# Second and third feed forward of a two-block layer stack: the up products with x held still and 512 weight columns moving, gated results turned on TensorE, and borders that go by quarters of x

## The chip, the core and the metric

The kernel runs on one core of one Trainium2 chip. A core has TensorE (PE in the profile; its weight loads are listed as PEld), VectorE (DVE), ScalarE (ACT), GpSimd (POOL) and SyncE (SP, which here only issues DMA). The metric is the device time of one execution in microseconds. The kernel before has a median of 3593.2 us over 3 runs (3590.34 to 3593.96).

## What is computed

Two blocks run one after the other on 256 rows (tokens) of 2048 columns, all in float32. The first block has a conditioned Fourier and mLSTM mixer and a feed forward with a convolution. The second has a feed forward, a mixer (a state space model beside sparse attention) and another feed forward. The change touches the two feed forwards of the second block, `f1` and `f2` below, called the second and the third feed forward of the kernel (n = 1 and n = 2):

```python
D_MODEL, SEQ, D_FF = 2048, 256, 5632

def _rmsnorm(x, g):
    xf = x.astype(jnp.float32)
    ms = jnp.mean(xf * xf, axis=-1, keepdims=True)
    return (xf * lax.rsqrt(ms + EPS)).astype(x.dtype) * g

def _swiglu(x, wg, wu, wd):
    return (jax.nn.silu(x @ wg) * (x @ wu)) @ wd

# second_block, the lines that matter here
f1 = _swiglu(_rmsnorm(h, ffn1_pre_g[l]), ffn1_w_gate[l], ffn1_w_up[l], ffn1_w_down[l])
h = h + 0.5 * _rmsnorm(f1, ffn1_post_g[l])
...
h = h + _rmsnorm(mixed, mix_post_g[l])
f2 = _swiglu(_rmsnorm(h, ffn2_pre_g[l]), ffn2_w_gate[l], ffn2_w_up[l], ffn2_w_down[l])
h = h + 0.5 * _rmsnorm(f2, ffn2_post_g[l])
```

## The kernel before

**Products in three parts.** Each float32 operand is split into a rounded part (`w_hi`, `xt_hi`, `hid_hi`) and the rest (`w_lo`, `xt_lo`, `hid_lo`). A product is hi·hi + hi·lo + lo·hi, three passes over the array.

**Weights stream in units of 1 MB.** A unit is 128 x 2048 elements. SP loads it into one of four slots of `stage`. ACT copies it to `w_hi` (`split`, L792), DVE subtracts to get `w_lo` (L1303), and both land in one of two halves of the split buffers. ACT may start on a unit only when PE has used up the unit two before it (`split_used`), and PE may start on a unit when DVE is done with it (`split_made`). SP reloads a slot when its unit is split. The order of the units is fixed by a plan that is worked out when the program is built (`plan[name]`, with the index of the first unit of each stage).

**The feed forward.** The 5632 hidden columns are 44 chunks of 128. They are done in two parts, 24 and 20 chunks (`PARTS`): the up products of a part (`up10`, `up11` of the second feed forward, `up20`, `up21` of the third), and then its down product (`down10` and so on). In the up products of before one unit holds 128 columns of the gate weights, or of the up weights, for all 2048 rows: 16 k chunks of 128 x 128. Two units, gate and up, make a pair, and there are 44 pairs in each feed forward. The weights are the stationary operand and x, turned so that its columns lie on the partitions, is the moving one (`wide_steps`):

```python
pe.matmul(dst, wh, both(k), start=k == 0, stop=False)                     # 512 columns: x_hi and x_lo of 256 rows
last = pe.matmul(dst[:, T:2 * T], wl, chunk(xt_hi, k), start=False, stop=False)  # 256 columns
```

The result is already turned: hidden columns on partitions and rows along the free axis, as the down product needs it. For each pair ACT copies a half of the banks (`e0`, L877), DVE adds the other (`d0`, L1499), multiplies by the row's reciprocal root, which was laid out along the free axis in `rsb` (`d1`, L1509), ACT takes the Silu (`e2`, L892), DVE multiplies gate and up (`d2`, L1532), and ACT and DVE split the result into `hid_hi` and `hid_lo` (`e3`, `d3`). Pairs run in hardware loops.

**The down product** (`rows_half`) has the other form: 128 rows of the turned hidden tile are stationary and 512 weight columns move; a unit is 256 rows of weights by 1024 columns. It is 24 matmuls of 512 columns a unit. Its last unit goes by quarters of the output (`quarters`, L2322 to L2324), so that the norm that follows can start on the first quarter.

**The borders.** Before the second feed forward the rows of x are made from the last down product of the first (`down01`), quarter by quarter: DVE (`add_gated`, `weigh_final`), then PE turns them (`norm(2, ...)`, L2384), and ACT and DVE scale and split them into `xt_hi` and `xt_lo` (`scaled_hi` L857, `scaled_lo` L1354). Before the third, the output product of the mixer (`out2`) has to be complete for its norm (`post_tail`); then `new_x(6, q)` (L1445) makes a quarter of x, `norm(4)` turns it, and so on. A unit of before needs all of x. `norm_done` counts the eight groups (two k chunks each) of x that are ready.

**The bias tables.** In the second feed forward PE also makes the bias tables of the attention (`bias_rows`, L2427 and L2431, 62 small matmuls); DVE copies them out (`take_bias`), and GpSimd writes them to memory with 16 transfers, of which each waits for a given number of used units.

## Time and profile before

| what | value |
|---|---|
| median of 3 runs | 3593.2 us |
| profiled execution: its time, its span | 3594.03 us, 3592.1 us |
| PE busy | 3425.2 us, 95% |
| PEld busy | 2919.4 us, 81% |
| DVE busy | 2130.7 us, 59% |
| ACT busy | 1636.2 us, 46% |
| granted TensorE clock, mean | 0.97 |
| second feed forward, up products of part one | from 1260.13 to 1553.45 us |
| third feed forward, first up matmul | 2836.82 us |

The table says how full each engine is, and where the two feed forwards lie. Busy time of PE comes from matmuls whose ends are modelled and overlap, so the spacing of starts, not the mean duration, is what one reads for its pace. A granted clock of 1.00 is 2.4 GHz, and 0.50 is 1.2 GHz.

### The profile page before, as it was taken

Reading aid. Unit: us, or ns where it says so; the run is one execution under the profiler, and the core shown is the slowest. Engines: PE = TensorE matmul, PEld = TensorE weight load, DVE = VectorE, ACT = ScalarE, POOL = GpSimd, SP = SyncE. Lnnn points to the kernel's source line nnn. Section 1 sums busy time; section 2 is a strip of 40 time slices with the busy share of each in tenths; the row PEclk is TensorE's granted clock in tenths of the full one; section 3 lists DMA queues with packets and bytes.
Section 4 is the critical chain, followed back from the end, with each engine's and each line's share of the span. In section 5 each row is a group of like instructions: output and inputs, shape, how many; then the busy total and the mean of one; then the engine's idle time right before and its main releaser. Section 6 shows DMA issues by size and latency. Waiting matters only on the chain.

```text
span 3592.1 us, 49777 instructions
## 1 busy us (share of the span) xinstructions
PE 3425.2 (95%) x19694; PEld 2919.4 (81%) x19694; DVE 2130.7 (59%) x2280; ACT 1636.2 (46%) x1772; POOL 346.2 (10%) x411
## 2 busy tenths in 40 slices
PE   5899889999999999999999899999999899999998
PEld 1786678888888888888888799898888788888886
DVE  0774657775566565544555578895455555545555
ACT  0333346653455455543443455663443555434443
POOL 1110000000000000000000147661000000000000
PEclk7899999999999999999999999999899999999999
DMA  9998657776666667976665656667235566666664
GB/s 398 297 340 299 221 167 225 225 227 221 188 187 195 189 186 164 204 206 189 187 187 188 175 149 156 168 179 232 91 106 187 153 187 186 187 189 188 185 188 139
DMA packets 813373, 712.54 MB, mean 198 GB/s; under 512 B 13127, under 2 KB 742527, under 8 KB 805696
## 3 DMA queue, kind: packets, MB, share of 16 engines
q1 hardware_dynamic: 787840, 627.09, 58.9%
q0 software_dynamic: 20624, 79.44, 7.8%
q10 hardware_dynamic: 4784, 4.27, 0.4%
q8 instruction: 88, 1.44, 0.2%
q14 instruction: 37, 0.30, 0.0%
HBM read 698.94 MB, written 11.80 MB: 198 GB/s over the span
## 4 chain that ended last, share of the span: by engine, by line
PE 78%; DVE 9%; ACT 4%; DMA 4%; issue 3%; POOL 1%; ACTq 0%; DVEq 0%; SPq 0%; POOLq 0%
PE ps L2267 24%; PE ps L2268 12%; PE ps L2335 8%; PE ps L2336 8%; PE ps L2339 8%; DVE w_lo L1303 3%; ACT w_hi L792 3%; DMA stage<-in_w_ada 2%; PE ps L2286 2%; PE ps L2287 2%; PE ps L2288 2%; PE ps L2265 2%; PE ps L2299 1%; PE ps L2495 1%; PE ps L2300 1%
## 5 line engine op out<-in xcount | busy, mean ns | idle before, releaser
L1303 DVE TENSOR_TENSOR w_lo<-stage,w_hi 128x2048 fp32r<-128x2048 f32 x528 | 1221.4, 2313 | 1093.7 <-ACT w_hi L792 1092.6
L792 ACT ACTIVATE w_hi<-stage 128x2048 fp32r<-128x2048 f32 x528 | 1010.8, 1914 | 1483.5 <-PE ps L2265 617.0
L2267 PE MATMUL ps<-xt,w_hi 128*128 128x512 f32 x3960 | 1416.2, 400 | 11.3 <-DVE w_lo L1303 10.1
L2268 PE MATMUL ps<-xt,w_lo 128*128 128x256 f32 x3960 | 1114.1, 281 | 0.0
L2267 PEld LDWEIGHTS ps<-xt,w_hi 128*128 128x128 f32 x3960 | 746.9, 189 | 187.8 <-DVE w_lo L1303 14.5
L2268 PEld LDWEIGHTS ps<-xt,w_lo 128*128 128x128 f32 x3960 | 750.9, 190 | 11.8
L2335 PE MATMUL ps<-w_hi,hid_hi 128*128 128x512 f32 x1152 | 449.2, 390 | 5.8 <-DVE w_lo L1303 5.8
L2336 PE MATMUL ps<-w_lo,hid_hi 128*128 128x512 f32 x1152 | 448.2, 389 | 0.0
L2286 PE MATMUL ps<-xt,w_hi 128*128 128x256 f32 x1184 | 342.2, 289 | 18.9 <-DVE w_lo L1303 16.6
L2339 PE MATMUL ps<-w_hi,hid_lo 128*128 128x512 f32 x1152 | 354.7, 389 | 0.0
L2287 PE MATMUL ps<-xt,w_hi 128*128 128x256 f32 x1184 | 337.0, 285 | 0.0
L2288 PE MATMUL ps<-xt,w_lo 128*128 128x256 f32 x1184 | 336.8, 284 | 0.0
L2335 PEld LDWEIGHTS ps<-w_hi,hid_hi 128*128 128x128 f32 x1152 | 216.2, 188 | 52.4 <-DVE w_lo L1303 4.3
L2286 PEld LDWEIGHTS ps<-xt,w_hi 128*128 128x128 f32 x1184 | 229.0, 193 | 29.8 <-issue 23.6
L2339 PEld LDWEIGHTS ps<-w_hi,hid_lo 128*128 128x128 f32 x1152 | 216.2, 188 | 45.0
L2336 PEld LDWEIGHTS ps<-w_lo,hid_hi 128*128 128x128 f32 x1152 | 216.3, 188 | 44.7
L2287 PEld LDWEIGHTS ps<-xt,w_hi 128*128 128x128 f32 x1184 | 229.3, 194 | 0.0
L2288 PEld LDWEIGHTS ps<-xt,w_lo 128*128 128x128 f32 x1184 | 229.1, 193 | 0.0
L2335 PE MATMUL ps<-w_hi,xt 128*128 128x512 f32 x248 | 98.4, 397 | 8.7 <-issue 3.2
L2265 PE MATMUL ps<-xt,w_hi 128*128 128x512 f32 x264 | 105.4, 399 | 0.0
L2495 PE MATMUL ps<-stage,csilu 128*32 128x512 f32 x384 | 68.3, 808 | 33.6 <-DMA stage<-in_w_ada 33.1
L2336 PE MATMUL ps<-w_lo,xt 128*128 128x512 f32 x248 | 97.2, 392 | 0.0
(414 smaller groups left out, 3649.9 us busy)
## 6 DMA issues: line engine op xcount, KB each, us to landing
stage<-in_w_in SPq DMA_DIRECT2D x92, 1024.0 KB, 5.7
stage<-in_w_up SPq DMA_DIRECT2D x88, 1024.0 KB, 5.8
stage<-in_ffn_w_gate SPq DMA_DIRECT2D x88, 1024.0 KB, 5.6
stage<-in_ffn_w_up SPq DMA_DIRECT2D x88, 1024.0 KB, 5.6
stage<-in_ffn_w_down SPq DMA_DIRECT2D x88, 1024.0 KB, 5.5
stage<-in_w_ada SPq DMA_DIRECT2D x48, 1024.0 KB, 8.8
stage<-in_w_down SPq DMA_DIRECT2D x44, 1024.0 KB, 5.1
late<-in_w_ada POOLq DMA_DIRECT2D x64, 512.0 KB, 6.7
```

The lines of the kernel that those rows point to most:

```text
L792: act.activation(w_hi[:, u % 2 * UNIT:(u % 2 + 1) * UNIT], slot(u % SLOTS), ACT.Copy).then_inc(hi_made, 1)
L1303: dve.tensor_tensor(w_lo[:, part], slot(u % SLOTS), w_hi[:, part].bitcast(F32), ALU.subtract).then_inc(split_made, 1)
L2265: last = pe.matmul(dst, wh, both(k), start=False, stop=True)
L2267: pe.matmul(dst, wh, both(k), start=k == 0, stop=False)
L2268: last = pe.matmul(dst[:, T:2 * T], wl, chunk(xt_hi, k), start=False, stop=False)
L2286: pe.matmul(dst, wh, chunk(xh, k0 + k), start=start and k == 0, stop=False)
L2287: pe.matmul(dst, wh, chunk(xl, k0 + k), start=False, stop=False)
L2288: last = pe.matmul(dst, wl, chunk(xh, k0 + k), start=False, stop=stop and k == n - 1)
L2335: pe.matmul(rows_cols(half, m, n, 512, swapped), a, wh, start=st, stop=False)
L2336: pe.matmul(rows_cols(half, m, n, 512, swapped), a, wl, start=False, stop=False)
L2339: last = pe.matmul(rows_cols(half, m, n, 512, swapped), b, wh, start=False, stop=en)
L2495: last = pe.matmul(ps[32 * j:32 * j + 32, b * 512:(b + 1) * 512], weight.to_broadcast([P, 32]), part[:, j % 2 * 512:(j % 2 + 1) * 512], st ...
```

## The change

It does four things in the second and third feed forward; the first feed forward keeps its form.

1. The up products take the form of the down product. A unit now holds 512 columns of gate (or up) weights for 4 k chunks (`blocks_of`). A block is 512 hidden columns, 8 units: gate and up in turn, for the four quarters of x. `BLOCKS` gives 6 and 5 blocks for the two parts, so there are still 88 units in each feed forward. In a unit each 128 x 128 piece of x is stationary and 512 weight columns move, 24 matmuls (`unit`). Results have rows on the partitions. A block takes four PSUM banks, and two blocks alternate.
2. The gating is done by block: Silu with the row's reciprocal root as scale (`gate`, ACT, 2 instructions), one product on DVE (`product`, 2 instructions), then PE turns the product, 8 transposes of 128 x 128 (`turn_hid`), after the second unit of the next block, and ACT and DVE split it (`hidden`, 2 instructions each). The layout of the root along the free axis goes (`rs_rows`, `take_rs`, `rsb`).
3. The borders go by quarters of x: the first two units need only its first quarter, and the transposes of the other quarters stand between the units (`norm_ffn1`, `norm_ffn2`). The orders on DVE and ACT follow.
4. The bias tables are made after unit 28 of `up10` (it was unit 11), and the loops over pairs and over the halves of the down product are written out.

```diff
+BLOCKS = tuple(chunks // 4 for _, chunks in PARTS)
...
+        def blocks_of(ws, f0):
+
+            views = [w.rearrange("(c k p) n -> c p k n", p=P, k=4) for w in ws]
+            return lambda i, u: [(slot(u % SLOTS).rearrange("p (k n) -> p k n", k=4),
+                                  views[u % 2][u // 2][:, :, ds(i * 512 + f0 * P, 512)])]
...
+                def gate(j):
+
+                    act.wait_ge(S["norm_rs"], ROOT_AT[RS_ROOT[n]] + 1)
+                    act.wait_ge(split_used, plan[up][1] + 8 * j + 9)
+                    for m in range(MT):
+                        at = RS_COL[n] + m
+                        last = act.activation(turn[:, m * 512:(m + 1) * 512], bank(block_bank(j, 0, m)), ACT.Silu,
+                                              scale=stats[:, at:at + 1])
+                    last.then_inc(S["pair_e2"], 1)
...
+                    if j and u == 0:
+                        gate(j - 1)
+                    elif j and u == 3:
+                        hidden(j - 1)
...
+                def product(j):
+
+                    dve.wait_ge(S["pair_e2"], block_at(n, part, j) + 1)
+                    dve.wait_ge(split_used, plan[up][1] + 8 * j + 10)
+                    for m in range(MT):
+                        at = RS_COL[n] + m
+                        last = dve.scalar_tensor_tensor(out=h_blk[:, m * 512:(m + 1) * 512],
+                                                        in0=bank(block_bank(j, 1, m)), scalar=stats[:, at:at + 1],
+                                                        in1=turn[:, m * 512:(m + 1) * 512], op0=ALU.mult, op1=ALU.mult)
+                    last.then_inc(S["pair_d2"], 1)
...
+                def unit(v):
+
+                    j, u = divmod(v, 8)
+                    pe.wait_ge(split_made, plan[up][1] + v + 1)
+                    for kk in range(4):
+                        k, at = 4 * (u // 2) + kk, v % 2 * UNIT + kk * 512
+                        wh, wl = (w[:, at:at + 512] for w in (w_hi, w_lo))
+                        for m in range(MT):
+                            dst = bank(block_bank(j, u % 2, m))
+                            pe.matmul(dst, chunk(xt_hi, k, m), wh, start=k == 0, stop=False)
+                            pe.matmul(dst, chunk(xt_hi, k, m), wl, start=False, stop=False)
+                            last = pe.matmul(dst, chunk(xt_lo, k, m), wh, start=False, stop=k == KC - 1)
+                    last.then_inc(split_used, 1)
+
+                def turn_hid(j):
+
+                    pe.wait_ge(S["pair_d2"], block_at(n, part, j) + 1)
+                    for c in range(4):
+                        for m in range(MT):
+                            last = pe.transpose(bank(block_bank(j, 0, c // 2), c % 2 * T + m * P, P),
+                                                h_blk[:, m * 512 + c * P:m * 512 + (c + 1) * P], ident[:, :])
+                    last.then_inc(S["hid_turned"], 1)
...
+                    unit(v)
+                    if part == 0 and j == 0:
+                        between(u)
+                    if j and u == 1:
+                        turn_hid(j - 1)
+                    if n == 1 and part == 0 and v == 28:
+                        bias_rows()
...
         def enter_ffn1(split):
 
             split(0)
+            square_pieces(2, x_nat, 1, 0, 4, 4)
             split(1)
-            square_pieces(2, x_nat, 1, 0, 4)
+            square_pieces(2, x_nat, 2, 0, 4, 6)
+            split(2)
             scaled_hi(2, 4, C_F1)
             scaled_hi(2, 5, C_F1)
...
-            new_x(6, 0)
-            new_x(6, 1)
-            scaled_lo(4, 0, C_F2)
-            scaled_lo(4, 1, C_F2)
-            split(1)
...
+            for q in range(4):
+                new_x(6, q)
+                if q == 3:
+                    dve.sem_inc(S["x_made"], 1)
+                scaled_lo(4, 2 * q, C_F2)
+                scaled_lo(4, 2 * q + 1, C_F2)
+                split(q + 1)
```

On PE, in the up products of the second feed forward, the order of before at the end of a unit and the start of the next is as follows (`xt` moves over `w_hi` or `w_lo`; L2267 is the matmul of 512 columns, L2268 that of 256, and L2264 and L2265 are those two of the last k chunk).

```order
L2268 MATMUL ps<-xt,w_lo 128x256
L2267 MATMUL ps<-xt,w_hi 128x512
L2268 MATMUL ps<-xt,w_lo 128x256
L2264 MATMUL ps<-xt,w_lo 128x256
L2265 MATMUL ps<-xt,w_hi 128x512
```

At the second unit of a block of the changed kernel, with the transposes of the block before, PE has these rows (L2581 to L2583 are the three passes of `unit`, L2591 is `turn_hid`).

```order
L2581 MATMUL ps<-w_hi,xt 128x512
L2582 MATMUL ps<-w_lo,xt 128x512
L2583 MATMUL ps<-w_hi,xt 128x512
L2591 MATMUL ps<-ident,h_blk 128x128 [waits pair_d2]
L2591 MATMUL ps<-ident,h_blk 128x128 x7
L2581 MATMUL ps<-w_hi,xt 128x512 [waits split_made]
L2582 MATMUL ps<-w_lo,xt 128x512
```

So all matmuls of a unit move 512 columns, and eight transposes that wait for DVE's product stand between two units once a block.

On DVE, at the start of the third feed forward, the order of before is this (L1445 is `new_x`, L1354 `scaled_lo`, L1303 the split of a unit).

```order
L1445 SCALAR_TENSOR_TENSOR x_nat<-f_nat,stats,x_nat 128x512 x4
L1354 SCALAR_TENSOR_TENSOR xt<-ps,cols,xt 128x256 x4
L1303 TENSOR_TENSOR w_lo<-stage,w_hi 128x2048
L1445 SCALAR_TENSOR_TENSOR x_nat<-f_nat,stats,x_nat 128x512 x2
L1354 SCALAR_TENSOR_TENSOR xt<-ps,cols,xt 128x256 x4
L1445 SCALAR_TENSOR_TENSOR x_nat<-f_nat,stats,x_nat 128x512 x2
L1354 SCALAR_TENSOR_TENSOR xt<-ps,cols,xt 128x256 x8
L1319 TENSOR_REDUCE stats<-stats 128x2
L1323 TENSOR_SCALAR stats<-stats 128x2
L1303 TENSOR_TENSOR w_lo<-stage,w_hi 128x2048
```

The same place in the changed kernel (L1509 is `new_x`, L1423 `scaled_lo`, L1372 the split):

```order
L1509 SCALAR_TENSOR_TENSOR x_nat<-f_nat,stats,x_nat 128x512 x2
L1423 SCALAR_TENSOR_TENSOR xt<-ps,cols,xt 128x256 x4
L1372 TENSOR_TENSOR w_lo<-stage,w_hi 128x2048
L1509 SCALAR_TENSOR_TENSOR x_nat<-f_nat,stats,x_nat 128x512 x2
L1423 SCALAR_TENSOR_TENSOR xt<-ps,cols,xt 128x256 x4
L1372 TENSOR_TENSOR w_lo<-stage,w_hi 128x2048
L1509 SCALAR_TENSOR_TENSOR x_nat<-f_nat,stats,x_nat 128x512 x2
L1423 SCALAR_TENSOR_TENSOR xt<-ps,cols,xt 128x256 x4
L1372 TENSOR_TENSOR w_lo<-stage,w_hi 128x2048
L1509 SCALAR_TENSOR_TENSOR x_nat<-f_nat,stats,x_nat 128x512 x2
L1423 SCALAR_TENSOR_TENSOR xt<-ps,cols,xt 128x256 x4
L1372 TENSOR_TENSOR w_lo<-stage,w_hi 128x2048 x2
```

Before, all four quarters were made with one split in between; now each quarter is made, scaled and followed by the split of one unit.

## Rows read from the trace of the kernel before

**Rows 1.** Page, part 1: busy us, share of the span, instructions.

```profile
PE 3425.2 (95%) x19694; PEld 2919.4 (81%) x19694; DVE 2130.7 (59%) x2280; ACT 1636.2 (46%) x1772; POOL 346.2 (10%) x411
```

**Rows 2.** Page, part 4: the chain that ended last, by engine.

```profile
PE 78%; DVE 9%; ACT 4%; DMA 4%; issue 3%; POOL 1%; ACTq 0%; DVEq 0%; SPq 0%; POOLq 0%
```

**Rows 3.** Groups by line: busy us, mean ns | idle before, releaser.

```profile
L2267 PE MATMUL ps<-xt,w_hi 128*128 128x512 f32 x3960 | 1416.2, 400 | 11.3 <-DVE w_lo L1303 10.1 <-issue 1.2
```

**Rows 4.** Timeline of PE, one unit of `up10`: start us, duration us.

```profile
1547.80 0.40 PE L2267 MATMUL ps<-xt,w_hi 128*128 128x512 f32 x1
...
1553.45 0.40 PE L2335 MATMUL ps<-w_hi,hid_hi 128*128 128x512 f32 x1
```

**Rows 5.** Timeline of PE, last unit of `down01` and the matmul after it.

```profile
1254.69 0.39 PE L2322 MATMUL ps<-w_hi,hid_hi 128*128 128x512 f32 x1
...
1260.13 0.39 PE L2267 MATMUL ps<-xt,w_hi 128*128 128x512 f32 x1
```

**Rows 6.** Timeline of PE, four transposes between two units of `down01`.

```profile
1242.39 0.62 PE L2339 MATMUL ps<-w_hi,hid_lo 128*128 128x512 f32 x2
1242.84 0.60 PE L2384 MATMUL ps<-ident,f_nat 128*128 128x128 f32 x4
1243.20 0.48 PE L2335 MATMUL ps<-w_hi,hid_hi 128*128 128x512 f32 x1
1243.52 0.39 PE L2336 MATMUL ps<-w_lo,hid_hi 128*128 128x512 f32 x1
```

**Rows 7.** Groups by line, 1400 to 1500 us, in `up10`.

```profile
L1303 DVE TENSOR_TENSOR w_lo<-stage,w_hi 128x2048 fp32r<-128x2048 f32 x18 | 41.3, 2292 | 43.7 <-ACT w_hi L792 43.7
L792 ACT ACTIVATE w_hi<-stage 128x2048 fp32r<-128x2048 f32 x18 | 34.5, 1916 | 46.5 <-PE ps L2265 46.5
...
L1499 DVE TENSOR_TENSOR turn<-turn,ps 128x512 f32<-128x512 f32 x9 | 6.1, 680 | 0.0
L877 ACT ACTIVATE turn<-ps 128x512 f32<-128x512 f32 x9 | 5.2, 577 | 0.0
...
L892 ACT ACT_TABLE_LOAD x4 | 5.1, 1283 | 0.1
```

**Rows 8.** Timeline of PE, start of the second feed forward: third and fourth unit.

```profile
1278.32 0.50 PE L2267 MATMUL ps<-xt,w_hi 128*128 128x512 f32 x1 [1.79 <-DVE w_lo L1303]
...
1289.83 0.39 PE L2265 MATMUL ps<-xt,w_hi 128*128 128x512 f32 x1
```

**Rows 9.** Timeline of DVE at the same border.

```profile
1265.29 1.28 DVE L1387 TENSOR_TENSOR f_nat<-ps,row 128x512 f32<-128x512 f32 x2
...
1267.93 1.29 DVE L1400 TENSOR_TENSOR f_nat<-x_nat,wf_row 128x512 f32<-128x512 f32 x2
```

**Rows 10.** Timeline of ACT at the same border.

```profile
1262.21 0.61 ACT L807 ACTIVATE turn<-x_nat 128x512 f32<-128x512 f32 x1
```

**Rows 11.** Timeline of DVE at the start of the third feed forward.

```profile
2823.32 2.86 DVE L1445 SCALAR_TENSOR_TENSOR x_nat<-f_nat,stats,x_nat 128x512 f32<-128x512 f32 x4
2826.88 1.66 DVE L1354 SCALAR_TENSOR_TENSOR xt<-ps,cols,xt 128x256 fp32r<-128x256 f32 x4 [0.70 <-ACT xt L857]
```

**Rows 12.** Timeline of PE there: first up matmuls, last matmul of unit four.

```profile
2836.82 0.78 PE L2267 MATMUL ps<-xt,w_hi 128*128 128x512 f32 x1
...
2838.25 0.63 PE L2267 MATMUL ps<-xt,w_hi 128*128 128x512 f32 x1
...
2840.81 0.57 PE L2267 MATMUL ps<-xt,w_hi 128*128 128x512 f32 x1
...
2863.28 0.40 PE L2265 MATMUL ps<-xt,w_hi 128*128 128x512 f32 x1
```

**Rows 13.** Windows: length, busy of PE, PEld, DVE, ACT, POOL, then PEclk, DMA share.

```profile
1210.00:1300.00 90.00, 84.97 (x425) 70.28 (x424) 66.20 (x69) 49.27 (x65) 7.61 (x13) 1.00 0.67 192
...
2837.00:2840.00 3.00, 3.00 (x11) 2.52 (x11) 1.73 (x4) 2.95 (x6) 0.00 (x0) 0.50 0.00 0
```

**Rows 14.** DMA issues: transfers of the bias tables, KB each, us to landing.

```profile
rev_scratch<-rev_sb POOLq DMA_DIRECT2D x16, 192.0 KB, 8.9
```

More of the change, by code:

```diff
@@ L890, in e2 @@
                     act.wait_ge(S["pair_d1"], j + (q0 + 3))
-                    src = conv_a[:, s * T:(s + 1) * T] if conv else turn[:, s * 512:s * 512 + T]
-                    act.activation(conv_a[:, s * T:(s + 1) * T], src, ACT.Silu).then_inc(S["pair_e2"], 1)
+                    here = conv_a[:, s * T:(s + 1) * T]
+                    act.activation(here, here, ACT.Silu).then_inc(S["pair_e2"], 1)
                 def e3(j, s):
@@ L903, in ffn, with ffn_rows, hidden @@
                     split_down(u)
+                    if part:
+                        after(u)
+        def ffn_rows(n, enter, after):
+            for part, (f0, chunks) in enumerate(PARTS):
+                up, down = f"up{n}{part}", f"down{n}{part}"
+                def gate(j):
[6 more added lines that the diff above has]
+                    last.then_inc(S["pair_e2"], 1)
+                def hidden(j):
+                    act.wait_ge(S["hid_turned"], block_at(n, part, j) - FC + 1)
+                    for b in range(2):
+                        at = (4 * j + 2 * b) * T
+                        act.activation(hid_hi[:, at:at + 512], bank(block_bank(j, 0, b)), ACT.Copy).then_inc(S["pair_e3"], 1)
+                for v in range(8 * BLOCKS[part]):
+                    if part or v > 4:
+                        split(up, 0, 0, v)
+                    elif v == 0:
+                        enter(lambda u: split(up, 0, 0, u))
+                    j, u = divmod(v, 8)
+                    if part == 0 and v == 5:
+                        root(RS_ROOT[n], 4 if n == 1 else 2)
+                    if j and u == 0:
+                        gate(j - 1)
+                    elif j and u == 3:
+                        hidden(j - 1)
+                for u in range(chunks):
+                    split(down, 0, 0, u)
+                    if u == 0:
+                        gate(BLOCKS[part] - 1)
+                    elif u == 3:
+                        hidden(BLOCKS[part] - 1)
                     if part:
@@ L1489, in ffn @@
                 pb = PAIR_BANK[part]
-                gating = n == 0 and part == 0
+                gating = part == 0
                 def split_down(u):
@@ L2471, in ffn @@
                     first_pairs()
-                if n == 1 and part == 0:
-                    pairs(1, 3)
-                    bias_rows()
-                    pairs(3, chunks // 2)
-                else:
-                    pairs(part == 0, chunks // 2)
-                if n == 0 and part:
+                pairs(part == 0, chunks // 2)
+                if part:
                     pe.wait_ge(S["mod_made"], 6)
                 rows_phase(f"down{n}{part}", chunks // 2, hid_hi, hid_lo, part == 0, q0 + 2, last=part == 1,
-                           after=turn_early if n == 0 and part else nothing)
+                           after=turn_early if part else nothing)
```

298 lines of the change are left out of this document (173 added, 125 removed).

## The prediction

> **What bounds the kernel now.** I read the page first. PE is busy 95% of the span, DVE 59%, ACT 46% [rows 1], and the chain that ended last runs through PE for 78% of its length [rows 2]. The groups by line then say where PE's own waits are: the matmuls of the up products, 3960 pairs, were held up 11.3 us in all [rows 3]. So inside the feed forwards PE never starves, and what counts is how long PE takes for a unit, and what it does beside units. The groups of a stretch inside `up10` say the same from the other side: ACT stood idle 46.5 us of 100 waiting for PE to free a buffer, and DVE 43.7 us waiting for ACT [rows 7]. Only at the borders does PE wait for the others.
>
> PE's pace I read from starts in its timeline, since the durations overlap. A unit of up products is 32 matmuls, and the starts at its two ends are 1547.80 and 1553.45: 5.65 us [rows 4]. The last unit of a down product goes in exactly the order that the changed `unit` has (hi·hi, hi·lo, lo·hi on one 128 x 128 piece of activations, 512 weight columns moving), and takes from 1254.69 to 1260.13: 5.44 us for 24 matmuls [rows 5]. Both move 12,288 columns (16 x 768 and 24 x 512).
>
> **1. The units.** 88 units in each of two feed forwards go from 5.65 to 5.44 us. That is 0.21 us each, and 176 x 0.21 = 37 us less. ACT's and DVE's part of a unit stays as it is: 1.92 + 2.29 = 4.21 us from the free buffer to the ready unit [rows 7], under the 5.44 us that PE needs for the unit in between. 1.2 us of slack are left, 0.2 less than before.
>
> The Trainium skill (TensorE: Matmul & The Clock Gate, section "Back-to-back issue gap") gives a warm matmul of N columns N/2.4 + 2.5 ns. By that a unit of before would take 5.20 us and a new one 5.18 us, the gain on all units would be about 4 us, and the whole sum about 1 us. The rows speak against it: both forms ran in this kernel, and differ by 0.21 us. I go by the rows.
>
> **2. The transposes.** They are new on PE: 8 for each of 22 blocks, 176 in all. Nothing hides them, since PE is the bound. Four such transposes between two units push the next matmuls: L2339's two start at 1242.39, so the next start is due at 1242.84; it comes at 1243.20, and the one after it another 0.32 us later where 0.23 is usual [rows 6]. That is 0.36 + 0.09 = 0.45 us for four. Eight cost between 0.81 us (the 0.09 paid once) and 0.91 us (twice the four). I take 0.91, so 22 x 0.91 = 20 us more; the low end is 18. Their wait for DVE's product costs nothing: gate and up of a block are done when the next block starts, Silu takes two ACT instructions of about 0.6 us, the product two DVE instructions of about 0.7 us (priced by L877 and L1499, the same 512 columns out of PSUM [rows 7]), the product is ready about 6 us into the block, and PE comes to the transposes after 10.9 us. The read-out after them needs four such instructions in all, and the banks are wanted again 6 units after the transposes, over 30 us later.
>
> **3. ACT and DVE** do less: four pairs of before are 16 DVE instructions and 12 on ACT, a block has 4 and 4 of at most the same width of 512. The table loads of 1.28 us each around every second Silu [rows 7] go with the loops, since code that is written out needs the table once. All of this lies beside PE and is priced at nothing. If it came late it would be worth its excess over the slack; see the third rival.
>
> **4. The border before the second feed forward.** Before, unit 0 starts at 1260.13 [rows 5], unit 2 only at 1278.32 after a wait for its split, and unit 3 ends 0.23 us after 1289.83, at 1290.06 [rows 8]. After: unit 0 starts at the same time, and now needs only the first quarter of x. It ends at 1265.6, and eight transposes make that 1266.5. Unit 1's split comes later than before, since ACT has its two squares (0.61 us and a read-out each [rows 10]) ahead of it; I estimate its start at 1262.6, so it is ready at 1266.8. Unit 1 runs to 1272.3. DVE makes the last quarter of x in 3.93 us (1265.29 to 1269.22 before [rows 9]), now 1266.8 to 1270.7; ACT squares and splits unit 2 behind that, ready at 1274.6: PE idles 1.4 us beside its transposes. Units 2 and 3 then run through to 1285.5. That is 4.6 us earlier, of which 4 x 0.21 are counted already: 3.7 us less.
>
> **5. The border before the third.** Before, DVE has the first quarter of x at 2824.7 and the second 1.4 us later (half of the 2.86 us), and the first four scaled pieces at 2828.54 [rows 11]. PE starts units only at 2836.82, with all quarters turned, and ends unit 3 at 2863.52 [rows 12]. It starts at the granted clock of 0.50, 1.2 GHz [rows 13]: from 2838.25 to 2840.81 four pairs take 0.64 us each, and then the clock rises, after some 4.4 us of dense matmuls [rows 12]. After: the first quarter is scaled at the same 2828.54, and unit 0 may start. I give it the same kind of low-clock start, 4.4 to 6 us at nearly double price, so it ends at about 2836.6. Now each further quarter goes through all engines in turn: PE turns it only between units, ACT and DVE scale it, ACT and DVE split a unit, and only then DVE makes the next quarter. Unit 1 ends at 2842.9; the third quarter is made at 2844.4, PE idles 1.5 us; unit 2 ends at 2850.9, the last quarter is made at 2852.3, again 1.5 us; unit 3 ends at 2858.8. That is 4.7 us earlier, 3.8 us beyond what is counted.
>
> **6. The bias tables** cost the same at their new place, tiny matmuls and a spell of half clock behind them. New is that GpSimd's transfers (16 of 192 KB, 8.9 us to landing [rows 14]) wait for unit counts that have mostly passed by then, so some six go at once. Weight loads have several units of slack by their slots; I price it at 0, at most 4 us.
>
> **Sum.** -37 (units) + 20 (transposes) - 3.7 - 3.8 (borders) = -25 us. The profiled execution took 3594.0 us (span 3592.1 and 1.9 around it), 0.8 above the median. 3594.0 - 25 = 3569, and 3569 stands for the median too.
>
> **Rivals.**
> - *The transposes take the clock down* (the slower side). At the start of the third feed forward, behind transposes that stood alone with gaps, it was 0.50 [rows 13]. Place: after the second unit of a block. A spell of 4.4 us in which a pair takes 0.64 instead of 0.35 us loses 2 us [rows 4, 12], so 22 spells lose 44: 3569 + 44 = 3613. It decides from 1.2 us per block. Against it: the stretch of 1210 to 1300 us has transposes in fours and eights at a granted 1.00 [rows 13]. 0.03. The Trainium skill (the same page, section "Part 4: PE-mode transpose") says transposes do not count as PE-busy in the same way; by that rule the clock would fall only if 0.9 us of them were enough, and here matmuls surround them.
> - *A unit is priced by its columns alone*, and the 0.21 us come from something else in the two places compared. Then units gain nothing, transposes and borders stay: 3594 + 20 - 7.5 = 3606. The equal 12,288 columns speak for it, the measured starts against [rows 4, 5]. 0.03. The skill's gap rule above is the same mechanism with cheaper transposes.
> - *Splits come late once a block.* ACT's `gate` lies between two splits. The room is 5.44 - 1.92 = 3.5 us, and the slack 1.2 on top; it would have to take over 4.7 us where I expect 1.2, or 3.8 with two table loads. Each 0.5 us of excess costs 22 x 0.5 = 11 us: 3580 to 3591. The same range holds a burst of bias transfers and borders that give nothing. 0.08.
> - *Cheaper still*: transposes by columns alone (8 x 128 at 0.44 ns each, 0.45 us, from 5.44 us for 12,288 [rows 5]) give 10 us more: 3559 or less. 0.06.
> - The forecast: 0.80.
>
> **Range and chances.** The forecast's own bounds: transposes 0.81 to 0.91 us and a little beyond, borders 0 to 10 us, transfers 0 to 4, which is 3563 to 3579. Toward the cases beside it I take 3560 to 3582. A measurement of this kernel tells 0.2%, 7 us, from no change: faster (below 3586) 0.90, same 0.04, slower 0.06, the two slow rivals.
>
> **What would show it.** In the changed kernel's profile: starts of `unit`'s matmuls 0.227 us apart and 5.44 us a unit; eight transposes (L2591) in 0.8 to 0.9 us with no idle time ahead of them for DVE; PEclk 1.00 through the up products except behind the bias tables; no ACT table loads inside blocks; the second feed forward's unit 4 near 1285.5 and the third's first unit about 8 us earlier relative to the end of `out2`. Wrong would be: units over 5.5 us, a wait for `h_blk` or `w_lo` once a block, half clock after L2591, or a wait on loads after the bias tables.

## The result, and the profile after

| | before | after |
|---|---|---|
| median of 20 runs each, same chip | 3596.36 us (3586.80 to 3598.49) | 3599.56 us (3593.99 to 3603.58) |
| ratio, with its 95% interval | | 1.0014 (1.0008 to 1.0020) |
| profiled execution, and its span | 3594.0, 3592.1 us | 3601.8, 3599.9 us |
| granted clock, mean | 0.970 | 0.966 |

The changed kernel is not faster. It is 3 us slower; the interval says that this is more than noise, and it lies inside the 0.2% that were called "same". 3569 us was forecast: 30 us are missing. The page of the changed kernel, its engines and its costliest groups:

```profile
PE 3412.2 (95%) x18458; PEld 2866.9 (80%) x18458; DVE 2017.5 (56%) x2010; ACT 1528.4 (42%) x1554; POOL 346.0 (10%) x411
...
L2581 PE MATMUL ps<-w_hi,xt 128*128 128x512 f32 x1408 | 553.2, 393 | 34.8 <-DVE w_lo L1372 32.9
L2583 PE MATMUL ps<-w_hi,xt 128*128 128x512 f32 x1408 | 550.4, 391 | 0.0
L2582 PE MATMUL ps<-w_lo,xt 128*128 128x512 f32 x1408 | 550.3, 391 | 0.0
```

All three engines did less work than before [rows 1], PE too, and still the span grew. The last column says where to look: the first matmul of a unit (L2581) was held up 34.8 us, where the one of before had 11.3 us [rows 3], and those 11.3 cover the first feed forward too, which keeps its form and has 6.2 us by itself in the changed kernel (L2371). The waits of PE, sorted, show that this is not spread over 176 units (columns: what was waited for, us in total, times, longest):

```profile
PE ps L2581 <- DVE w_lo L1372: 32.9, 3, 31.4
```

One wait of 31.4 us. The timeline around it, of all engines but PE's matmuls in a row (columns: start, us, then in brackets the idle time before and who ended it):

```profile
1438.18 0.55 POOL L565 DMA_DIRECT2D bias_scratch<-bias_sb  x1 [125.85 <-DVE bias_sb L1613]
1438.72 2.60 POOL L568 DMA_DIRECT2D rev_scratch<-rev_sb  x5
1440.25 0.37 SPq L358 DMA_DIRECT2D stage<-in_ffn_w_gate  x1
...
1445.09 0.52 POOL L568 DMA_DIRECT2D rev_scratch<-rev_sb  x1 [3.78 <-PE ps L2583]
...
1449.16 3.14 SPq L358 DMA_DIRECT2D stage<-in_ffn_w_up  x1
...
1454.74 8.39 SPq L358 DMA_DIRECT2D stage<-in_ffn_w_gate  x1
...
1463.30 29.87 SPq L358 DMA_DIRECT2D stage<-in_ffn_w_up  x1
...
1494.54 1.91 ACT L812 ACTIVATE w_hi<-stage 128x2048 fp32r<-128x2048 f32 x1 [36.85 <-DMA stage<-in_ffn_w_gate]
1496.48 2.29 DVE L1372 TENSOR_TENSOR w_lo<-stage,w_hi 128x2048 fp32r<-128x2048 f32 x1 [35.15 <-ACT w_hi L812]
...
1498.83 0.79 PE L2581 MATMUL ps<-w_hi,xt 128*128 128x512 f32 x1 [31.40 <-DVE w_lo L1372]
```

Read it from the bottom up. PE waits for DVE's low half, DVE for ACT's high half, and ACT 36.85 us for a weight load. At the top stands what came just before: five bias transfers in one go, the sixth 4 us later. Two more follow at 1455.97 and 1466.85, at gates of their own, and queue up behind them: they take 35 and 30 us to land. The loads' queue (SPq) takes 0.37 us to issue a load at 1440.25, and 29.87 us at 1463.30. What the DMA engines did meanwhile is in the windows (columns: stretch, its us, busy us and instructions of PE, PEld, DVE, ACT and POOL, granted clock, DMA share, GB/s):

```profile
1440.00:1450.00 10.00, 10.00 (x43) 8.20 (x42) 2.37 (x2) 1.92 (x1) 1.84 (x4) 0.94 0.98 29
1450.00:1460.00 10.00, 10.00 (x46) 8.29 (x45) 4.57 (x3) 4.99 (x4) 0.52 (x1) 1.00 0.93 32
...
1480.00:1490.00 10.00, 0.00 (x0) 0.00 (x0) 0.00 (x0) 0.00 (x0) 0.00 (x0) 0.50 0.95 90
...
1497.00:1502.00 5.00, 3.17 (x8) 2.50 (x9) 4.00 (x3) 2.88 (x3) 0.00 (x0) 0.50 0.95 357
```

The engines are busy for 93 to 98% of the time and move 29 to 32 GB/s; over the whole span they moved 198. Behind the wait PE starts at a granted 0.50 (1.2 GHz). The DMA view of 1420 to 1475 us says whose the time was (queues: packets, MB, share; issues: KB each, median us to landing):

```profile
q0 software_dynamic: 386, 1.27, 60.4%
q1 hardware_dynamic: 1360, 2.72, 14.5%
...
stage<-in_ffn_w_gate SPq DMA_DIRECT2D x3, 1024.0 KB, 45.6
stage<-in_ffn_w_up SPq DMA_DIRECT2D x3, 1024.0 KB, 39.7
rev_scratch<-rev_sb POOLq DMA_DIRECT2D x8, 192.0 KB, 29.6
```

GpSimd's queue holds 60% of the engines' time for 1.27 MB. A weight load of 1 MB takes 40 to 46 us to land, against 5.1 us as the median of all 88 of `ffn_w_gate`.

Everything else went as forecast, which the section on the prediction takes up. The rows for it are unit 4 from its first three matmuls to the start of unit 5, and the eight transposes of a block:

```profile
1287.87 0.39 PE L2581 MATMUL ps<-w_hi,xt 128*128 128x512 f32 x1
1288.10 0.39 PE L2582 MATMUL ps<-w_lo,xt 128*128 128x512 f32 x1
1288.33 0.39 PE L2583 MATMUL ps<-w_hi,xt 128*128 128x512 f32 x1
...
1293.31 0.39 PE L2581 MATMUL ps<-w_hi,xt 128*128 128x512 f32 x1
...
1320.52 1.03 PE L2591 MATMUL ps<-ident,h_blk 128*128 128x128 f32 x8
1321.31 0.47 PE L2581 MATMUL ps<-w_hi,xt 128*128 128x512 f32 x1
1321.62 0.39 PE L2582 MATMUL ps<-w_lo,xt 128*128 128x512 f32 x1
```

### The profile page after: what moved, and what is told of

It is laid out like the page before. It is cut to its first block, busy times and chain, and to the rows that moved or that the text cites. A ratio compares the mean times of both kernels' runs of the same rounds, so it can differ in the third digit from the quotient of the medians.

```text
span 3599.9 us, 45279 instructions
## 1 busy us (share of the span) xinstructions
PE 3412.2 (95%) x18458; PEld 2866.9 (80%) x18458; DVE 2017.5 (56%) x2010; ACT 1528.4 (42%) x1554; POOL 346.0 (10%) x411
## 4 chain that ended last, share of the span: by engine, by line
PE 78%; DVE 9%; ACT 5%; DMA 4%; issue 3%; another core or an unknown queue 1%; POOL 1%; ACTq 0%; DVEq 0%; SPq 0%; POOLq 0%
PE ps L2581 9%; PE ps L2583 9%; PE ps L2582 9%; PE ps L2439 8%; PE ps L2440 8%; PE ps L2443 8%; PE ps L2371 7%; DVE w_lo L1372 4%; PE ps L2372 3%; ACT w_hi L812 3%; DMA stage<-in_w_ada 2%; PE ps L2390 2%; PE ps L2391 2%; PE ps L2392 2%; PE ps L2403 1%
## 5 line engine op out<-in xcount | busy, mean ns | idle before, releaser
L1372 DVE TENSOR_TENSOR w_lo<-stage,w_hi 128x2048 fp32r<-128x2048 f32 x528 | 1221.4, 2313 | 1211.3 <-ACT w_hi L812 1210.6
L2581 PE MATMUL ps<-w_hi,xt 128*128 128x512 f32 x1408 | 553.2, 393 | 34.8 <-DVE w_lo L1372 32.9
L2583 PE MATMUL ps<-w_hi,xt 128*128 128x512 f32 x1408 | 550.4, 391 | 0.0
L2582 PE MATMUL ps<-w_lo,xt 128*128 128x512 f32 x1408 | 550.3, 391 | 0.0
L2371 PE MATMUL ps<-xt,w_hi 128*128 128x512 f32 x1320 | 473.1, 401 | 6.2 <-DVE w_lo L1372 6.2
L2372 PE MATMUL ps<-xt,w_lo 128*128 128x256 f32 x1320 | 371.7, 282 | 0.0
L2390 PE MATMUL ps<-xt,w_hi 128*128 128x256 f32 x1184 | 342.7, 289 | 18.5 <-DVE w_lo L1372 15.8
L2581 PEld LDWEIGHTS ps<-w_hi,xt 128*128 128x128 f32 x1408 | 266.1, 189 | 90.8 <-DVE w_lo L1372 31.6
L2392 PE MATMUL ps<-xt,w_lo 128*128 128x256 f32 x1184 | 337.4, 285 | 0.0
L2583 PEld LDWEIGHTS ps<-w_hi,xt 128*128 128x128 f32 x1408 | 265.8, 189 | 55.8
L2582 PEld LDWEIGHTS ps<-w_lo,xt 128*128 128x128 f32 x1408 | 266.1, 189 | 54.8
L2371 PEld LDWEIGHTS ps<-xt,w_hi 128*128 128x128 f32 x1320 | 249.3, 189 | 67.0 <-DVE w_lo L1372 9.7
L2372 PEld LDWEIGHTS ps<-xt,w_lo 128*128 128x128 f32 x1320 | 250.5, 190 | 3.6
L2390 PEld LDWEIGHTS ps<-xt,w_hi 128*128 128x128 f32 x1184 | 229.5, 194 | 29.8 <-issue 23.4
```

What stands on the lines that cost most here:

```text
L1372: dve.tensor_tensor(w_lo[:, part], slot(u % SLOTS), w_hi[:, part].bitcast(F32), ALU.subtract).then_inc(split_made, 1)
L2390: pe.matmul(dst, wh, chunk(xh, k0 + k), start=start and k == 0, stop=False)
L2581: pe.matmul(dst, chunk(xt_hi, k, m), wh, start=k == 0, stop=False)
L2582: pe.matmul(dst, chunk(xt_hi, k, m), wl, start=False, stop=False)
L2583: last = pe.matmul(dst, chunk(xt_lo, k, m), wh, start=False, stop=k == KC - 1)
```

## The experiments

To compare traces without what happens ahead of the change, one measure is used throughout: the stretch from the first to the last matmul of the last units of the down products (L2322 before, L2426 after). It is 2322.3 us before and 2328.0 us after, 5.7 more. The runs lie on several chips; each ratio is to the kernel before on the same chip, and medians are subtracted only where they come from one chip (experiments 1 to 4, 5 to 8, 10 and 11).

**Theory A:** the new units, transposes and borders give the 25 us as forecast, and a burst of bias transfers takes them away. In the changed kernel the bias rows come after unit 28, when the unit counts that the first transfers wait for have passed. **Theory B:** the new form itself is at fault (its order, its code, its splits), and the stall is only where it shows.

### 1. The bias rows earlier

```diff
-                    if n == 1 and part == 0 and v == 28:
+                    if n == 1 and part == 0 and v == 12:
                         bias_rows()
```

DVE's copy goes from unit 29 to 13 and PE's wait for it from block 4 to 2. The gates of the sixteen transfers stay, and now each one is still to come.

> The changed kernel with the bias tables made after unit 12 of up10 and not after unit 28, so that GpSimd's 16 transfers of 192 KB start before their unit counts have passed and go one at a time, every second unit, as in the kernel before. Theory A (the burst of transfers starves the weight loads, and that alone eats the gain): the wait of 31.4 us on a weight load and some 1.7 us at half clock behind it go, and the kernel is 22 to 30 us faster than the one before (3566 to 3575 us). Theory B (the unrolled form or the new loads are slow in themselves, and the burst only shows it): a wait on stage of more than 10 us stays somewhere in up10, and the time is within 10 us of before.

Measured: 3570.47 us (3567.68 to 3571.07), ratio 0.9936 (0.9922 to 0.9949). The stretch is 2297.3 us, 25.0 less than before. The wait is gone:

```profile
L2581 PE MATMUL ps<-w_hi,xt 128*128 128x512 f32 x1408 | 552.5, 392 | 3.4 <-DVE xt L1423 1.8 <-DVE w_lo L1372 1.5
```

### 2. The bias rows late, the transfers paced

```diff
-            pool.wait_ge(split_used, plan["up10"][1] + 22 + 2 * h)
+            pool.wait_ge(split_used, plan["up10"][1] + 32 + 7 * h // 4)
```

> The changed kernel with the bias tables at their new place (after unit 28), but the transfers paced: they wait for 32, 33, 35, 37, 39 ... 58 used units, one every 1.75 units, in place of 22, 24 ... 52. Theory A (the burst): as fast as the version with early tables, within 4 us, and no wait of ACT on a weight load. Theory B (the late place of the tables itself costs, by DVE held up in take_bias or by the half clock in the middle): some 33 us stay, near 3600 us.

Measured: 3566.37 us (3565.23 to 3569.36), ratio 0.9928 (0.9913 to 0.9944), stretch 2297.0 us. So the late place does no harm, only the burst does.

### 3. The kernel before, with such a burst

```diff
-            pool.wait_ge(split_used, plan["up10"][1] + 22 + 2 * h)
+            pool.wait_ge(split_used, plan["up10"][1] + max(22 + 2 * h, 32))
```

> The kernel before with one change: the first five transfers of the bias tables wait for 32 used units as the sixth does, so six go at once. Theory A (a burst of transfers out of one partition starves whatever weight load there is): a wait of PE of 20 to 40 us in up10 with the old form as well, 3615 to 3635 us. Theory B (the new loads with 2 KB pieces, or the shorter unit, are what makes the queue fall behind): less than 8 us over the kernel before.

Measured: 3628.02 us (3627.28 to 3629.89), ratio 1.0100 (1.0085 to 1.0116), stretch 2354.5 us, 32.2 more. In the old form PE stands as long as in the new one:

```profile
PE ps L2267 <- DVE w_lo L1303: 41.1, 15, 30.9
```

Runs 1 to 3 settle A against B: the burst costs 31 to 32 us of the stretch in either form (2328.0 - 2297.0 and 2354.5 - 2322.3), and without it the new form gives 25 us.

### 4. Each transpose twice

```diff
-                    for c in range(4):
+                    for c in (0, 1, 2, 3) * 2:
```

On top of experiment 1. It tells what the transposes cost by more than one row.

> The version with early bias tables, with each of the 176 transposes of the gated results done twice (into the same place, so the result is the same). It prices the transposes. Theory A (nothing hides them, 0.1 us each): 22 x 8 more at 0.09 to 0.11 us, 16 to 20 us slower than the version with early tables. Theory B (part of them lies in a wait that is there anyway, or the clock falls on a longer row of transposes): less than 8, or more than 35 us.

Measured: 3586.81 us (3583.88 to 3589.84), ratio 0.9984 (0.9975 to 0.9994). That is 16.3 us above experiment 1, for 22 x 8 more transposes: 0.74 us a block, 0.093 us each. In the traces the two feed forwards themselves take 19.1 us longer, 0.87 us a block, and the stretch between them, which the edit does not touch, 2.2 us less. So eight more transposes cost 0.87 us where they stand, and part of it comes back elsewhere. The granted clock behind sixteen of them stays at 1.00 (window of the three us that hold the sixteen of the first block):

```profile
1319.00:1322.00 3.00, 3.00 (x23) 2.73 (x22) 0.21 (x1) 2.16 (x2) 0.00 (x0) 1.00 0.62 191
```

### 5 and 6. The transfers in twos and in fours

```diff
-            pool.wait_ge(split_used, plan["up10"][1] + 22 + 2 * h)
+            pool.wait_ge(split_used, plan["up10"][1] + 22 + 4 * (h // 2))
```

On top of experiment 1; experiment 6 has `8 * (h // 4)`. There are as many transfers, over nearly the same stretch of time.

> The kernel of the first experiment (bias rows after unit 12), with the sixteen bias tables' transfers let go in twos, every fourth unit, instead of one at every second unit; as many in all. Theory of the burst (eight transfers at once took some 53 us to come out and the weight loads had about 12 us of slack): two at once keep the loads back by about 13 us, just about the slack, so PE stands 0 to 4 us and the time is 3570 to 3576 us. Rival, each transfer costs its share however it comes (31 us for sixteen): no change from the first experiment, 3570. Rival, any two together are a burst: 3580 or more.

> The same with the transfers let go in fours, every eighth unit. Theory of the burst: four at once keep the loads back by 26 us and more against 12 of slack, so PE stands some 10 to 14 us behind the first group, and again behind each later one unless the slack is back by then: 3580 to 3610 us, the wait at the up units' first matmul on the low half of a split. Rival, only the number counts: 3570 us. Rival, the eight of the changed kernel are needed before anything is late: 3570 to 3573.

Measured: in twos 3569.57 us (3565.49 to 3571.74), ratio 0.9924 (0.9908 to 0.9941), and no wait of PE is listed from 1280 to 1640 us. In fours 3619.78 us (3617.33 to 3620.98), ratio 1.0066 (1.0049 to 1.0082). PE's waits of 1280 to 1640 us in the latter:

```profile
PE ps L2581 <- DVE w_lo L1372: 32.6, 3, 11.2
PE ps L2439 <- DVE w_lo L1372: 10.5, 1, 10.5
```

That is 10 us above the top of what was expected for fours. Four bursts, four waits, each about 11 us and 43.1 us together. A burst of two fits into what the loads are ahead, one of four does not. Four small bursts cost more than the single large one: the stretch is 2345.1 us, 47.8 above experiment 1, where the changed kernel's was 30.7 above. Unit by unit against experiment 1 the delay is 52.7 us at the end of the second feed forward: the four waits, and 1.7 to 2.8 us each time in what follows the wait, where the granted clock is 0.50 to 0.67. The stretch between the feed forwards is 4.9 us shorter and gives that much back. The time to landing of a bias transfer grows with the group: at most 9.2 us alone (experiment 1), 15.8 in twos, 29.5 in fours, 39.5 in the burst of the changed kernel.

### 7. The same burst, read from 128 partitions

```diff
-            pool.dma_start(rev_dram[h:h + 1], rev_sb[h:h + 1, :].unsqueeze(1).to_broadcast([1, P, 384])).then_inc(S["rev_out"], 16)
+            pool.dma_start(rev_dram[h], x_nat[:, 0:384]).then_inc(S["rev_out"], 16)
```

The changed kernel with its burst, but with another source; the content of the bias tables is left out by it. A transfer of before writes one partition's 1.5 KB row 128 times; here it reads 128 partitions once.

> The changed kernel with its late burst kept, but each bias transfer reads its 192 KB from 128 partitions (384 numbers of each of x's rows) and not 128 times from one partition; the bias tables' content is left out by that, size, pieces of 1.5 KB, queue and times of issue stay. If it is the reading of one partition over and over that makes the burst slow, the eight land within some 20 us, PE stands under 12 us and the time is 3572 to 3583 us. Rival, the bytes or the number of pieces or the queue they come in are what starves the loads: PE stands 28 to 34 us and the time stays at 3597 to 3603 us.

Measured: 3570.39 us (3566.16 to 3570.75), ratio 0.9927 (0.9910 to 0.9944). The burst is still issued, and costs nothing: the time is that of experiment 1, 1.6 us below the bottom of what was expected. The issue of the first five, and the windows:

```profile
1437.24 2.68 POOL L568 DMA_DIRECT2D rev_scratch<-x_nat  x5
```

```profile
1440.00:1450.00 10.00, 10.00 (x44) 8.21 (x43) 2.29 (x1) 2.73 (x2) 0.54 (x1) 0.97 0.60 190
1450.00:1460.00 10.00, 10.00 (x45) 8.28 (x45) 5.72 (x4) 4.17 (x4) 0.54 (x1) 1.00 0.66 220
```

190 and 220 GB/s stand where the changed kernel had 29 and 32, at a DMA share of 0.60 to 0.66 instead of 0.93 to 0.98. The DMA view of 1420 to 1475 us, in the same columns as above:

```profile
q0 software_dynamic: 576, 1.82, 8.9%
...
stage<-in_ffn_w_gate SPq DMA_DIRECT2D x3, 1024.0 KB, 5.8
rev_scratch<-x_nat POOLq DMA_DIRECT2D x8, 192.0 KB, 4.1
```

GpSimd's queue moves more (1.82 MB against 1.27) in a seventh of the share. So neither bytes, nor their number of packets (1712 of that queue in both kernels between 1200 and 1640 us), nor the queue, nor the moment is what hurts, but the source: one partition's row, read 128 times. Experiments 10 and 11 ask what of it.

### 8. The third border in another order

In the trace of the changed kernel PE waits for x behind units 1 and 2 (1.29 and 1.30 us), and DVE, which makes x, had stood idle 6.47 us shortly before (brackets):

```profile
2844.68 1.97 PE L2488 MATMUL ps<-ident,x_nat 128*128 128x128 f32 x8 [6.55 <-DVE x_nat L1509]
2848.49 0.80 PE L2581 MATMUL ps<-w_hi,xt 128*128 128x512 f32 x1 [1.84 <-DVE xt L1423]
...
2858.43 1.66 DVE L1423 SCALAR_TENSOR_TENSOR xt<-ps,cols,xt 128x256 fp32r<-128x256 f32 x4 [6.47 <-ACT xt L877]
...
2872.49 1.06 PE L2488 MATMUL ps<-ident,x_nat 128*128 128x128 f32 x8 [1.30 <-DVE x_nat L1509]
```

Experiment 8 is the second experiment with another order: DVE makes quarters 0 and 1 of x first, and quarters 2 and 3 right behind the first split. PE turns four groups ahead of unit 0, two behind it, two behind unit 1 (it was two ahead and two behind each of three units).

```diff
+            new_x(6, 0)
+            new_x(6, 1)
             for q in range(4):
-                new_x(6, q)
-                if q == 3:
-                    dve.sem_inc(S["x_made"], 1)
                 scaled_lo(4, 2 * q, C_F2)
                 scaled_lo(4, 2 * q + 1, C_F2)
                 split(q + 1)
+                if q == 0:
+                    new_x(6, 2)
+                    new_x(6, 3)
+                    dve.sem_inc(S["x_made"], 1)
...
-        norm(4, range(2))
+        norm(4, range(4))
...
-            if u < 3:
-                norm(4, range(2 + 2 * u, 4 + 2 * u))
+            if u < 2:
+                norm(4, range(4 + 2 * u, 6 + 2 * u))
```

> The second experiment (transfers paced out) with the third feed forward's border written otherwise: DVE makes x's first two quarters before the first low halves and the other two right behind the first split, and PE turns four groups before unit 0 and two each behind units 0 and 1. In the changed kernel's trace PE stands 1.29 and 1.30 us for quarters 2 and 3 of x behind units 1 and 2 while DVE stands idle for 6.47 us before them. If those waits are on the path: 2.5 to 3 us less than the second experiment, ratio to the kernel before about 0.992, and no wait on x_nat behind units 0 and 1. Rival, the waits only move to the low halves that follow: within 0.5 us of the second experiment.

Measured: 3562.60 us (3558.11 to 3566.55), ratio 0.9905 (0.9888 to 0.9921), the fastest of all kernels run. The intervals of experiments 2 and 8 overlap, so the gain is read from the traces: the stretch is 2290.7 us, 6.3 less than 2297.0. That is twice the 3 us expected, because of a second effect (L2491 and L2584 are L2488 and L2581 of the changed kernel, three lines further down):

```profile
2816.32 3.36 PE L2491 MATMUL ps<-ident,x_nat 128*128 128x128 f32 x16 [6.55 <-DVE x_nat L1509]
...
2820.13 0.50 PE L2584 MATMUL ps<-w_hi,xt 128*128 128x512 f32 x1 [0.45 <-DVE xt L1423]
...
2825.70 1.03 PE L2491 MATMUL ps<-ident,x_nat 128*128 128x128 f32 x8
```

Sixteen transposes in place of eight bring PE almost without a gap to unit 0 (0.45 us against 1.84). They start at a granted 0.50, the clock rises while they run, and unit 0 begins at 2820.13 at 1.00:

```profile
2816.00:2819.00 3.00, 2.68 (x13) 2.68 (x14) 2.27 (x5) 1.52 (x4) 0.00 (x0) 0.50 0.85 322
2819.00:2820.00 1.00, 0.68 (x5) 0.44 (x3) 1.00 (x4) 0.99 (x4) 0.00 (x0) 0.89 0.02 8
2820.00:2825.00 5.00, 4.87 (x21) 4.05 (x22) 4.96 (x6) 0.75 (x3) 0.00 (x0) 1.00 0.27 68
```

Unit 0 takes 5.57 us (2820.13 to 2825.70). In experiment 2 it takes 8.38 (2813.44 to 2821.82), and in the changed kernel 8.36. It starts no sooner than there, 10.7 us behind the last matmul of `out2` in both. So the 6.3 us are 2.6 of the two waits, 2.8 of unit 0 at full clock, and some 0.8 of one row of transposes fewer between units.

### 9. The kernel before, its transfers from 128 partitions

The edit of experiment 7 in the kernel before, which lets one transfer go at every second unit. Here too the content of the bias tables is left out.

> The kernel before with its sixteen bias transfers reading 384 numbers of 128 rows of x in place of one partition 128 times (the bias tables' content is left out; size, pieces, queue and times of issue stay: one at every second up unit). If a single transfer out of one partition is already hidden when it comes alone: within 0.2% of the kernel before, 3588 to 3600 us, and the 11.3 us that PE stands at the up units' first matmul stay as they are. Rival, each one holds a weight load back a little and the kernel before paid for it too: 3 to 9 us less, with those 11.3 us falling to 3.

Measured: 3595.12 us (3589.12 to 3601.02) beside 3596.77, ratio 0.9998 (0.9990 to 1.0007), and L2267's idle time is 11.3 us as before. A transfer that comes alone, even out of one partition, costs nothing that can be measured.

### 10 and 11. The same burst, read from four partitions

Both are the changed kernel with its burst. Each transfer reads four partitions of x, 32 times each; in 10 they are 0 to 3, in 11 they are 0, 4, 8 and 12 (`x_nat[0:16:4, 0:384]`). The content of the bias tables is left out. The edit of 10:

```diff
-            pool.dma_start(rev_dram[h:h + 1], rev_sb[h:h + 1, :].unsqueeze(1).to_broadcast([1, P, 384])).then_inc(S["rev_out"], 16)
+            pool.dma_start(rev_dram[h].rearrange("(a b) c -> a b c", a=4), x_nat[0:4, 0:384].unsqueeze(1).to_broadcast([4, 32, 384])).then_inc(S["rev_out"], 16)
```

> The changed kernel with its burst, each bias transfer reading partitions 0 to 3 of x, 32 times each (the bias tables' content is left out; bytes, rows of 1.5 KB, queue and times of issue stay). Theory P, it is one partition that is slow to read: four partitions are read side by side, a transfer lands within some 4 us and the burst costs under 8 us: 3570 to 3578 us. Theory Q, neighbouring partitions share one way out: a transfer alone still takes 8 to 9.5 us to land, as from one partition, the burst costs 20 to 33 us and the time is 3590 to 3603 us. The Trainium skill (SBUF — State Buffer, section "Door 1: The DMA port swizzle") is for Q: it puts partitions 0 to 3 on one port and gives a port 27 GB/s.

> The same with partitions 0, 4, 8 and 12 of x, 32 times each: again four partitions, the same pieces and the same spread over the queue's engines, but a distance of four between them. Theory P: as the run on partitions 0 to 3, whatever that gives. Theory Q: the ways out are now different ones, a transfer lands in 3 to 5 us and the burst is harmless or nearly so, 3568 to 3578 us, 15 to 30 us under the run on partitions 0 to 3. Should both stand near 3600, what matters is that a transfer is spread over fewer than 16 engines or that rows are read many times, and the port has nothing to do with it. The Trainium skill's page of the other run puts these four on four ports.

Measured: with 0 to 3, 3599.72 us (3597.01 to 3605.90), ratio 1.0020 (1.0011 to 1.0030). With 0, 4, 8 and 12, 3565.67 us (3564.30 to 3569.32), ratio 0.9928 (0.9912 to 0.9945). PE's wait for the low half with 0 to 3 (27.2 of the 28.7 us lie between 1280 and 1640 us, where with 0, 4, 8 and 12 there is none; the other 1.5 belong to the borders, as in experiment 1), and behind it the DMA view of 1420 to 1475 us of that kernel:

```profile
PE ps L2581 <- DVE w_lo L1372: 28.7, 4, 17.3
```

```profile
q0 software_dynamic: 1080, 1.19, 55.4%
...
stage<-in_ffn_w_gate SPq DMA_DIRECT2D x2, 1024.0 KB, 40.9
rev_scratch<-x_nat POOLq DMA_DIRECT2D x8, 192.0 KB, 32.7
```

The same view with 0, 4, 8 and 12:

```profile
q0 software_dynamic: 1600, 1.83, 16.4%
...
stage<-in_ffn_w_gate SPq DMA_DIRECT2D x3, 1024.0 KB, 5.6
rev_scratch<-x_nat POOLq DMA_DIRECT2D x8, 192.0 KB, 8.7
```

Only the distance between the four partitions differs, and it decides over 34 us. Reading a row many times is not it either: both read each row 32 times. That is theory Q: neighbours share one way out of SBUF, and it is this way, not the single partition, that the burst fills. The transfers that came alone agree. From 1505 us on a transfer of experiment 10 lands in 9.8 to 10.9 us, as slow as one out of one partition (8.7 to 9.2 us), and one of experiment 11 in 5.5 to 7.1 us. The two fell a little outside what Q expected (8 to 9.5 and 3 to 5 us), and so did the time of experiment 11, by 2.3 us to the fast side. The first transfer of the burst landed in 2.6 and 2.9 us in the two runs; why it was so quick stays open. The Trainium skill (SBUF — State Buffer, section "Door 1: The DMA port swizzle") has the rule: partitions 0 to 3 lie on one port, 27.2 GB/s each port. The trace comes near it: 22 GB/s for a transfer alone out of one partition, and in the burst 29 and 32 GB/s for all DMA, the loads among it. Why the other queue's loads stand behind such a transfer is in the skill only for writes between cores (DMA: Bandwidth & Descriptors, section "Back-pressure in remote DMA": stalled writes stall the engine's other queues too). Here it is seen for reads out of SBUF: loads of 40 us beside DMA engines that are 93 to 98% busy. That the engines are held in the same manner is not shown.

## Why the prediction was wrong

It fell by one step, the sixth, on the bias tables: "some six go at once. Weight loads have several units of slack by their slots; I price it at 0, at most 4 us." The count was nearly right (five at once, the sixth 4 us later, and two more before these were out), the price was not: 31.4 us of PE standing, and 1.8 us in the unit behind it, which starts at half clock. Two things were wrong in it. First, the slack was counted in slots of the buffer and never in time. Experiments 5 and 6 bracket it: two transfers at once (the last lands 15.8 us after issue) are hidden, four (29.5 us) cost 11 us of standing. Second, a transfer was priced as one of its kind had run alone, 8.9 us to landing [rows 14], and nothing was asked about what the DMA engines do in that time. A row on that could have been read: 192 KB in 8.9 us are 22 GB/s, a ninth of the 198 that the whole kernel moves. By that, six at once could hold a load back by up to 6 x 8.9 = 53 us, an estimate and the upper bound to state. The burst was even named among the rivals, at 11 to 22 us, but only in a bundle with other causes and 0.08.

What the transfers share is shown by experiments 7, 10 and 11: the way out of a few neighbouring partitions.

So the forecast's other terms have to be read without the burst, from experiment 1. This table has the time on PE from the last matmul of one product to that of the next, in us:

| | second feed forward (`down01` to `down11`) | between (`down11` to `out2`) | third (`out2` to `down21`) |
|---|---|---|---|
| before | 758.8 | 799.1 | 759.6 |
| experiment 1 | 744.5 | 800.5 | 747.6 |
| experiment 2 | 744.6 | 800.2 | 747.5 |
| after | 778.0 | 797.7 | 747.5 |

The other steps, each with what it measured:

- **Units.** Forecast 5.44 us. Starts are 0.227 us apart, and unit 4 runs from 1287.87 to 1293.31, 5.44 us; the splits on ACT follow in the same step, from 1450.33 to 1455.77. Right, -37 us. By the formula that the Trainium skill (TensorE: Matmul & The Clock Gate, section "Back-to-back issue gap") gives for the gap of one matmul by itself, this term would have been nearly nothing; the rows of both forms decide against it here, since 25 us come out (experiments 1 and 2).
- **Transposes.** Forecast 0.91 us a block, at least 0.81. Before the next unit starts they take 1321.31 - 1320.52 = 0.79 us, and that unit takes 5.57 us instead of 5.44 (1321.31 to 1326.87): 0.92 us, so 22 x 0.92 = 20.2 us. The group of L2591 over all 176 has no idle time ahead of it. Eight more cost 0.87 us (experiment 4). The granted clock is 1.00 from 1355 to 1540 us of experiment 1 and from 2874 to 3440 us of the changed kernel: the slow rival is out.
- **Splits, gates, products.** No wait once a block: L2581 was held up 3.4 us in all in experiment 1. L2267 had 5.0 us in the same two feed forwards (3.8 for the low half, 1.2 of issue).
- **The border before the second feed forward.** Forecast -3.7 us. From the start of the last matmul of `down01` to the end of unit 3: before 1259.90 to 1290.06, 30.16 us; after 1262.03 to 1287.87, 25.84. That is 4.3 less, 0.84 of it in the units: -3.5. Before, unit 4 had to wait too, and started only at 1290.66; after, it follows at once: -4.1 in all.
- **The border before the third.** Forecast -3.8 us, with gaps of 1.5 us. From the last matmul of `out2` to the end of unit 3: before 2817.85 to 2863.52, after 2837.74 to 2878.87. 45.67 - 41.13 = 4.5, less 0.84: -3.7. The gaps were 1.29 and 1.30 us.
- **The bias rows.** Forecast nothing. Before, they put 14.1 us between two units (from the last matmul of unit 11 to that of unit 12 it is 19.70 us, where a unit takes 5.65); at the new place units 28 and 29 take 12.6 us more than two units (experiment 2). That is -1.5, which the forecast did not have.

The sum of the measured terms is -37 + 20.2 - 4.1 - 3.7 - 1.5 = -26.1 us; the two feed forwards of experiment 1 shrank by 14.3 and 12.0, 26.3 us. The stretch between them, which holds none of the changed units, grew by 1.3, and so 25.0 came out. That the forecast said exactly 25 is partly luck: the bias rows, the wait before unit 4 and the stretch between are small terms that it had at nothing, and they partly cancel. In the changed kernel the second feed forward is 33.5 us longer than in experiment 2: 31.6 up to the start of the unit that waited, 1.8 in that unit. The stretch between gives 2.5 back, 31.0 in all. Why this stretch moves between 797.7 and 800.5 us stays open.

## What to carry to other kernels

Ask of each transfer not only when it lands, but what share of the DMA engines it holds and for how long. One that moves 22 GB/s (here 128 copies out of one partition) is harmless alone and held up the weight loads' queue in a burst; wait for counts that pace it, or spread its source over partitions that do not share a way out (0, 4, 8 and 12 here, or all 128). When work moves later in a program, look at everything that waits for it and has a gate of its own: gates that have passed turn a paced series into a burst. And where PE must restart from an idle clock, filling the gap ahead of the first costly matmul with work that is due anyway (experiment 8) was worth as much at this border as taking out the two waits.

## What the runs showed of the hardware

- A transfer of 192 KB by GpSimd's queue takes 8.7 to 9.2 us to land alone when it reads one partition 128 times, and 2.1 to 6.2 us, the burst included, when it reads 128 partitions once (experiments 1 and 7).
- Read from partitions 0 to 3 the burst has PE stand 27.2 us, from 0, 4, 8 and 12 not at all, with a ratio of 1.0020 against 0.9928 (experiments 10 and 11).
- In the burst the DMA engines were 93 to 98% busy at 29 to 32 GB/s, and a 1 MB load's issue took 29.87 us of its queue's time instead of 0.37.
- Eight 128 x 128 fp32 transposes between matmuls cost 0.92 us, eight more 0.87, and the granted clock stayed at 1.00. Behind an idle spell sixteen of them started at 0.50 at 2816.32, and in the window from 2820 us on it was 1.00 (experiment 8).
